# Small float32 products of a hybrid decoder kernel: each cut into four products of 32 stationary columns

## What is computed

```python
c_act = silu(c)
for l in range(2):
    mod = c_act @ w_mod[l] + b_mod[l]            # 6 vectors of 1024 per layer
    h = x * (1 + sc1) + sh1
    y = hybrid_mixer(h, w_in[l], ..., w_out[l])  # indexer + top-64 attention (8 heads x 64), gated linear attention (4 heads)
    x = layer_norm(alpha * x + (1 + g1) * y)
    h = x * (1 + sc2) + sh2
    y = swiglu(h, dense weights) if l == 0 else top-2-of-8 experts of swiglu(h)
    x = layer_norm(alpha * x + (1 + g2) * y)
```

## Time and profile before

| | us |
|---|---|
| median of 3 runs (lowest, highest) | 1355.04 (1354.43, 1355.78) |
| the profiled execution, its own time | 1353.39 |
| its span, first to last instruction | 1351.7 |
| PE busy | 1235.5 (91%) |
| PEld busy | 683.6 (51%) |
| DVE busy | 555.8 (41%) |
| ACT busy | 318.5 (24%) |
| mean granted TensorE clock | 0.965 of full speed |

### The profile page before, as it was taken

One profiled execution on the slowest core, in us unless ns is written; L12 is line 12 of the kernel. 1 busy time (PEld: TensorE's weight loads), 2 busy tenths in 40 slices (PEclk: granted clock), 3 DMA queues, 4 the chain that ended last, 5 costly groups with the idle time before them and its releaser, 6 DMA issues.

```text
span 1351.7 us, 24041 instructions
## 1 busy us (share of the span) xinstructions
PE 1235.5 (91%) x10082; PEld 683.6 (51%) x10082; DVE 555.8 (41%) x846; ACT 318.5 (24%) x552; POOL 43.5 (3%) x86
## 2 busy tenths in 40 slices
PE   2899979999979996899999899999899999999992
PEld 2888967778858885533334223333233333333331
DVE  5899886877668996420020110210200200210206
ACT  0656142344236551220021100101100101100102
POOL 2101010000010001000000000000000000000001
PEclk9999989999989998899999999999899999999996
DMA  9954778798518459489989969989789989999830
GB/s 341 319 169 156 254 262 291 291 387 297 166 49 258 162 189 402 170 297 407 413 328 405 361 234 412 408 332 382 308 313 411 389 351 378 368 381 413 328 124 32
DMA packets 149075, 403.47 MB, mean 298 GB/s; under 512 B 19964, under 2 KB 71328, under 8 KB 137696
## 3 DMA queue, kind: packets, MB, share of 16 engines
q1 hardware_dynamic: 146720, 395.16, 78.1%
q0 software_dynamic: 2240, 6.68, 1.4%
HBM read 400.75 MB, written 1.05 MB: 297 GB/s over the span
## 4 chain that ended last, share of the span: by engine, by line
PE 69%; DVE 6%; issue 2%; DMA 1%; ACT 1%; POOL 0%; POOLq 0%; SPq 0%; DVEq 0%; ACTq 0%
PE bank L1268 33%; PE bank L1292 17%; PE bank L325 3%; PE bank L327 3%; PE bank L326 3%; PE bank L1302 1%; PE bank L1248 1%; PE bank L1273 1%; PE bank L1256 1%; DVE u_low L1479 1%; DVE mod_acc L1468 1%; DMA raw_u<-in_ffn_w_up_dram 1%; PE bank L1257 1%; DVE stats L1492 1%; PE bank L968 1%
## 5 line engine op out<-in xcount | busy, mean ns | idle before, releaser
L1268 PE MATMUL bank<-raw_w,xg 128*32 128x512 f32 x4096 | 462.7, 598 | 10.2 <-issue 10.2
L1268 PEld LDWEIGHTS bank<-raw_w,xg 128*32 128x32 f32 x4096 | 127.8, 110 | 273.3 <-issue 271.2
L1292 PE MATMUL bank<-raw_w,heT 128*32 128x512 f32 x2112 | 232.9, 593 | 0.6 <-ACT heT L848 0.6
L1830 DVE TENSOR_TENSOR he<-he,bank 128x256 f32<-128x256 f32 x64 | 23.3, 417 | 384.9 <-ACT he L837 384.9
L1292 PEld LDWEIGHTS bank<-raw_w,heT 128*32 128x32 f32 x2112 | 66.9, 110 | 149.4 <-issue 147.5
L837 ACT ACTIVATE he<-bank 128x256 f32<-128x256 f32 (+1 forms) x72 | 21.4, 370 | 414.9 <-PE bank L1268 284.0
L1857 DVE SCALAR_TENSOR_TENSOR ycat<-bank,gate_tab,ycat 128x512 f32<-128x512 f32 x36 | 25.5, 747 | 198.5 <-PE bank L1257 198.5
L1468 DVE SCALAR_TENSOR_TENSOR mod_acc<-mod_row,c_act,mod_acc 128x1024 f32<-128x1024 f32 x70 | 89.9, 1284 | 9.5 <-DMA mod_row<-in_w_mod_dram 3.9
L325 PE MATMUL bank<-u_high,hT_H 128*128 128x256 f32 x256 | 74.2, 290 | 3.0 <-DVE u_low L1479 3.0
L327 PE MATMUL bank<-u_high,hT_L 128*128 128x256 f32 x256 | 72.2, 282 | 0.0
L326 PE MATMUL bank<-u_low,hT_H 128*128 128x256 f32 x256 | 72.0, 281 | 0.0
(11 more groups left out here) (288 smaller groups left out, 1561.0 us busy)
## 6 DMA issues: line engine op xcount, KB each, us to landing
raw_w<-in_moe_w_down_dram SPq DMA_DIRECT2D x88, 1024.0 KB, 8.4
raw_w<-in_moe_w_gate_dram SPq DMA_DIRECT2D x128, 512.0 KB, 7.4
raw_w<-in_moe_w_up_dram SPq DMA_DIRECT2D x128, 512.0 KB, 8.7
mod_row<-in_w_mod_dram SPq DMA_DIRECT2D x80, 512.0 KB, 6.7
raw_w<-in_moe_w_gate_dram SPq DMA_DIRECT2D x64, 384.0 KB, 3.6
raw_w<-in_moe_w_up_dram SPq DMA_DIRECT2D x64, 384.0 KB, 4.6
u_raw<-in_w_in_dram SPq DMA_DIRECT2D x20, 1024.0 KB, 7.3
raw_d<-in_ffn_w_down_dram SPq DMA_DIRECT2D x11, 1024.0 KB, 10.1
```

The costliest lines, as they stand in the source:

```text
L1268: last = mm(bank[m // 4][32 * q:32 * q + 32, :].rearrange("s (m f) -> s m f", m=2), xg[:, i, k, 32 * g:32 * g + 32], W[:, :, a * 256:(a + ...
L1292: last = mm(bank[3 + g][32 * q:32 * q + 32, :], heT[:, i, at:at + 32], W[:, b, h * 512:(h + 1) * 512], start=(c == 0 and a == 0), stop=(c ...
L1830: last = V.tensor_tensor(he[:, b, :], he[:, b, :], bank[b][:, 256:512], ALU.mult)
```

## The change

A helper `mm4` takes the place of `mm` in the products listed above. It issues four products with 32 stationary columns each, one per column quarter, with the same moving operand; the signal stands on the last of them. So one product, two load and matmul pairs in the trace, becomes four, eight pairs.

```diff
+            def mm4(out_ap, lhsT, rhs, start, stop):
+
+                for q in range(4):
+                    p = slice(32 * q, 32 * q + 32)
+                    last = mm(out_ap[p], lhsT[:, p], rhs, start=start, stop=stop)
+                return last
...
-                    last = mm(o[:, k:k + 1], acc[:, k * P:(k + 1) * P], ones[:, 0:1], start=True, stop=True)
+                    last = mm4(o[:, k:k + 1], acc[:, k * P:(k + 1) * P], ones[:, 0:1], start=True, stop=True)
...
-                                last = mm(b[:, T + t * 72:T + (t + 1) * 72], hfull[:, kt, t * P:(t + 1) * P], W[:, kt, P:KW],
+                                last = mm4(b[:, T + t * 72:T + (t + 1) * 72], hfull[:, kt, t * P:(t + 1) * P], W[:, kt, P:KW],
...
-                            last = mm(o[:, 2 * pr:2 * pr + 2, q0:q0 + BLK], kfac[:, pr, tb, j, :],
+                            last = mm4(o[:, 2 * pr:2 * pr + 2, q0:q0 + BLK], kfac[:, pr, tb, j, :],
...
-                    last = mm(bank[2][:, h * 64:(h + 1) * 64], pT0[:, h, :], av[:, 0, :], start=True, stop=True)
+                    last = mm4(bank[2][:, h * 64:(h + 1) * 64], pT0[:, h, :], av[:, 0, :], start=True, stop=True)
...
-                    mm(bank[1][:, e], pT1[:, 2 * h, :], av[:, 0, :], start=True, stop=False)
-                    last = mm(bank[1][:, e], pT1[:, 2 * h + 1, :], av[:, 1, :], start=False, stop=True)
+                    mm4(bank[1][:, e], pT1[:, 2 * h, :], av[:, 0, :], start=True, stop=False)
+                    last = mm4(bank[1][:, e], pT1[:, 2 * h + 1, :], av[:, 1, :], start=False, stop=True)
...
-                    last = mm(bank[(7, 5)[t]][:, 0:NE], hfull[:, kt, t * P:(t + 1) * P], wr[:, kt, :],
+                    last = mm4(bank[(7, 5)[t]][:, 0:NE], hfull[:, kt, t * P:(t + 1) * P], wr[:, kt, :],
```

More of the change, by code:

```diff
@@ L991, in project @@
                             for kt in range(KT):
-                                last = mm(b[:, T + t * 72:T + (t + 1) * 72], hfull[:, kt, t * P:(t + 1) * P], W[:, kt, P:KW],
-                                          start=(kt == 0), stop=(kt == KT - 1))
+                                last = mm4(b[:, T + t * 72:T + (t + 1) * 72], hfull[:, kt, t * P:(t + 1) * P], W[:, kt, P:KW],
+                                           start=(kt == 0), stop=(kt == KT - 1))
                 last.then_inc(s["proj"], 1)
@@ L1059, in mixer @@
                             q0 = j * BLK
-                            last = mm(o[:, 2 * pr:2 * pr + 2, q0:q0 + BLK], kfac[:, pr, tb, j, :],
-                                      qfP[:, pr, :, tb * P + q0:tb * P + q0 + BLK], start=True, stop=True)
+                            last = mm4(o[:, 2 * pr:2 * pr + 2, q0:q0 + BLK], kfac[:, pr, tb, j, :],
+                                       qfP[:, pr, :, tb * P + q0:tb * P + q0 + BLK], start=True, stop=True)
                     last.then_inc(s["at_ps"], 1)
@@ L1235, in _ @@
             sel = rt[8]
[L1236 to L1240, removed]
+            mm4(bank[7][:, 16:24], upper[:], sel[:, 0, :], start=True, stop=True)
+            mm4(bank[7][:, 24:32], ones[:, 0:P], sel[:, 0, :], start=True, stop=False)
+            mm4(bank[7][:, 24:32], upper[:], sel[:, 1, :], start=False, stop=True)
+            mm4(bank[7][:, 32:40], ones[:, 0:P], sel[:, 0, :], start=True, stop=False)
+            mm4(bank[7][:, 32:40], ones[:, 0:P], sel[:, 1, :], start=False, stop=True).then_inc(s["rank_ps"], 1)
             def gather(r, b=6):
```

## The result

The changed kernel took 1341.49 us, the median of 6 runs (1338.71 to 1343.11), beside 1354.74 us for the kernel before on the same chip. The ratio is 0.9895 with an interval of 0.9867 to 0.9923: 14.2 us faster by the ratio, where the forecast was 8.9 and the range ended at 1342.5. The sign was right, the size was not.

The account below looks back on a forecast made before the run. Mixers alternate between PE and DVE, PE fills the dense layer, and the changed products are bound by 128-column weight loads; the experts' 780 us only shift. Seven parts sum to 8.9 us, giving 1346.1 us, range 1342.5 to 1355.

Parts of the forecast that it names:

- part 3: Values in mixer 0: shorter products end DVE's 0.88 us wait and start transposes earlier; gain 1.3 us, between 0.9 and 3.1.
- part 2: Keys and linear attention blocks in mixer 0: only DVE's 1.3 us wait for head products can go; gain 1.0 us.
- Part 1: Second sum at the start, which DVE waits for: 0.9 us on quarters instead of 2.06; gain 1.2 us.
- Parts 2 to 4: Mixer 0: keys with linear attention blocks, values, and sums; gains of 1.0, 1.3 and 0.9 us.
- first rival: DVE and transfers take back mixer gains from keys, linear blocks and values, and half of three dense sums: 1350.3 us; chance 0.17.
- part 4: Sums in mixer 0: the one after i = 2 gains 0.9 us, the one after i = 3 nothing.
- Part 5: Sums in the dense layer: steps 5, 6 and 8 gain 3 x 0.9 = 2.7 us; step 3 is absorbed by waits.
- Part 6: Mixer 1: DVE is full, only its 0.5 us wait for head products goes; gain 0.5 us.
- Part 7: Router and ranks: router gains 0.28 us, ranks 0.7, and 0.3 more from the transposes ahead; together 1.3 us.
- No round narrower than 0.115 us: Rival: sums on quarters take 2.14 us against 1.7, small products lose; about +2 us, 1357; chance 0.12.
- supply of instructions: Rival: PE's instruction supply limits the change at 0.041 us per record, decisive point 0.014; about 1377; chance 0.08 for both forms.
- milder form: Of the instruction supply rival: a fetch runs dry; three 3.01 us stalls on the path would eat the gain; chance within 0.08.

Follow-up runs that it names:

- unrolled kernel before: The kernel before with the first two of three passes of PE's loop over pairs of experts written out, products unchanged, against the kernel before: 1338.55 us, ratio 0.9868.

## Why the prediction was wrong

**The step that failed** is the first one: "None of the changed products is there, so the change can only shift this stage, not shorten it", and with it "The experts' 780 us should be unchanged". The products are not there, but their instructions are in the same stream as the loop. The stage is 7.3 us shorter because the changed kernel puts a block's end elsewhere behind the loop's head. Two kernels show it without the products: 60 instructions ahead of the loop bring 6.5 us to the kernel before, and 196 take 8 to 9 us from the changed one, of which the tiny products themselves were put at 1.0. I had seen the stall after the jump and used it for a rival, as something that the change might add; I had not looked at the second stall eight matmuls later, nor asked on what it depends. As a term it measured 7.3 us: with it the forecast would have been 1338.8 instead of 1346.1, against the 1341.49 measured.

The Trainium skill (Runtime: NRT & Kernel Launch, section Instruction fetch mechanics) says that instructions are brought in blocks of 256, strictly in order, and that a taken branch to a target that is not at hand waits for its block. The runs agree: 2.6 to 3.7 us after each jump, and a period that fits 256 and not 128. That the second wait is for the next block is the reading that fits all seven counts; no trace shows the fetch itself.

**The products** brought some 7 us where the sum had 8.9: 6.9 by the shifts of the one pair of profiles, once the 0.5 us from before the first sum are off. The forecast's range had its lower end at 1342.5, 12.5 us below the median of before; its parts with 3.1 us in part 3 and the whole 1.3 us wait in part 2 add up to 11.0, so that end had no full sum. By the parts, always for this one pair of executions:

- Part 1, second sum at the start: 0.9 for 1.2. It took 1.17 us from PE's start to DVE's reading (forecast 0.9, before 2.06). PE also began it at 30.80 and not 31.32, but that is the 0.5 us of DVE's accumulations at 8 us, ahead of both sums, and not their work. And the gain was not kept: at 43.8 us DVE's next weight split came 1.4 us later than before, as ACT waited 3.4 us for a unit of w_in where it had waited 0.9, and at 67 us the shift was -0.3.
- Parts 2 to 4, mixer 0: 1.2 for 3.2. This is the mis-sized term. Keys and linear blocks hold PE for 2.2 and 2.0 us, as forecast, and the 1.3 us wait for the head products is gone, which takes the shift to -1.7 at 94 us. I can't put that to the change, though: the unrolled kernel before, whose products are the old ones, has no such wait either, and keys and linear with the passes written out still wait 0.6 us. By the values the shift is used up:

```profile
131.41 3.56 PE L923 MATMUL bank<-av,pT 128*32 128x64 f32 x128 [0.81 <-ACT pT L722]
...
134.25 2.29 DVE L1486 TENSOR_TENSOR u_low<-u_raw,u_high 128x2048 fp32r<-128x2048 f32 x1
136.45 0.20 DVE L1617 RECIPROCAL rinv<-rsum 128x8 f32<-128x8 f32 x1
```

  DVE's split starts at 134.25, 0.29 us later than before, though all before it was 1.7 us early at 94. DVE's waits in mixer 0 say who took it back, after and then before: rows of w_mod.

```profile
DVE mod_acc L1475 <- DMA mod_row<-in_w_mod_dram: 3.1, 2, 2.0
```
```profile
DVE mod_acc L1468 <- DMA mod_row<-in_w_mod_dram: 1.0, 1, 1.0
```

  That is the first rival's mechanism, at work in this one stage; but the unrolled kernel before waits 1.9 us there with the old products, so how much of it the change causes is not shown. The wait of 0.88 us for the values is gone, as forecast, and PE still waits 0.81 us for ACT ahead of them, as before. The values took 3.56 us and not 2.2 because half clock now fell at 131.3 to 134.7; their rounds start 0.107 us apart, twice the 0.056 of the 64-column rounds at full clock. From there the shorter values take the shift to -1.7 at 141 us, 2.0 for the 1.3 of part 3, and the sum after i = 2 takes it to -2.6, the 0.9 of part 4. So what was mis-sized is not the products' gains but what the transfers leave of them: 1.4 us were lost by 67 us and 2.0 by 126 us.
- Between 166 and 258 us 1.0 was given back, which no part had. It goes to the transfers of the dense weights: ACT's waits for them are 7.9 us where they were 5.0 (gate weights, 230 to 262 us), and the split of 254 us comes only 0.3 us earlier than before.
- Part 5, the dense layer: 2.6 for 2.7. PE is still without a gap there:

```profile
276.60:374.00 97.40, 97.40 (x615) 78.63 (x614) 65.77 (x67) 32.77 (x42) 0.00 (x0) 1.00 0.76 265
```

- Part 6, from 344 us through mixer 1 to the router's reading: 0.5 + 1.6 = 2.1, for 0.5 and the router's 0.28. DVE's waits for head products (0.5) and for the router (0.28) are gone, as forecast; the rest no part had, and in the profile where the ranks were read at 548.10 it isn't there.
- Part 7, ranks: 1.1 for 1.0. PE's start to DVE's reading is 0.65 us instead of 1.59, at 542.61 and 543.26.

**The rivals.** No round narrower than 0.115 us is out: it is 0.032 to 0.034 for one column and 0.062 for 72. With it goes the estimate by the Trainium skill (TensorEngine Tiling (Array Packing), section Performance Considerations), 0.10 us per round: here the 64 matmuls of a sum were all done in 0.71 us, so the quarters do not pay a fixed 60 cycles one after the other (the page's rule, so read, does not hold in this trace). The supply of instructions has no limit near 0.014 us per record: the sum's 128 records take 0.64 us, 0.005 each. And the milder form, a fetch that decides, did decide, with the sign that I had not allowed. DVE and the transfers took back the start's gain by 44 us, 2 us at the values of mixer 0 and 1 after it, not half of the dense sums. So this rival was right for mixer 0; that the total still came near its forecast owes something to gains in mixer 1 that no part had.

**What stays open.** Keys and linear blocks alone cost 4 to 7 us once the loop's part is taken out, and in the whole change they don't show as a loss. The parts alone therefore don't add up to the whole. In keys and linear blocks together, in which nothing of the loop's part is gained, it is 4.6 us. The way in which the router's stage is clocked is worth 4 to 5 us and fits in size, it was seen in four of eight profiles with a plain router and in none of six with one on quarters, and the granted clock over all runs points the same way. But one profile a kernel can't tell how often each way occurs in one and the same kernel, and the times of the runs made to test it overlap.

## What to carry to other kernels

A kernel with a loop has a term that no product has: where its head stands in the blocks of 256 instructions. Before reading a gain of half a per cent as the work of a change, compare the stretch that the change doesn't touch, and its waits for issue; a few idle instructions ahead of the loop, or the passes written out, tell the two apart, and here writing them out alone was worth at least as much as the change (0.9868 and 0.9895, with intervals that overlap). A shift between one pair of traces needs the same care: the same code up to the ranks differed by 5 us between profiles. Small float32 products with few moving columns took the same time for 1 as for 72 columns, 0.22 us each, which fits their 128-column weight loads as the bound; on four column quarters the same product took 0.07 to 0.12.

## What the runs showed of the hardware that I had not expected

- After a jump back PE had nothing to do for 2.6 to 3.7 us, and for another 2.1 to 4.1 us, eight pairs later, where 0, 768 or 2560 instructions more stood ahead of the loop. With the half clock behind them the two jumps cost the kernel before 15.3 us, by the experts' stage with the passes written out (796.75 less 781.4).
- Adding 60 instructions made the kernel 6.5 us faster by the ratio.
- Four matmuls of one column on four quarters follow each other in 0.034 us, loads included; before, one load and matmul pair on the whole array took 0.105.
- The same stage of the same work, at the router, ran either at mixed clock (0.73 before) or at 0.51 (the unrolled kernel before), 4 to 5 us apart, in kernels that differ only far from it.
